# A transformer pair on one Trainium2 core: the last 128 tokens' expert gathers in two halves of 64, and the first half's second block computed together with token block 2

## The chip, the cores and the metric

The program runs on one core of one Trainium2 chip, in float32 throughout. The metric is the device time of one execution in microseconds (us). Before the change it is 1934.56 us, the median of 3 runs (1934.11 to 1935.18).

The engines are named as in the profile: PE (TensorE, the matmuls) and PEld (its weight loads), DVE (VectorE), ACT (ScalarE), POOL (GpSimd, here only the issuer of indirect gathers), SP (SyncE, the issuer of all other transfers).

## The reference, cut to what matters

512 tokens of width 1024 go through two blocks. The first block mixes tokens (attention and a gated recurrence) and then runs a product-key expert layer. The expert layer is what the gathers serve:

```python
def one_block(xb):                                   # 128 tokens
    q = einsum(xb, w_query)                          # 8 heads x 2 x 128
    s = einsum(q, subkeys)                           # scores against 2 x 128 keys
    ... # two top-16 and a top-16 of their 256 sums: 16 experts per head, of 16384
    u = u_table[experts]                             # 128 experts per token, 1024 floats each
    hid = gelu(einsum('nkd,nd->nk', u, xb)) * gates
    return einsum('nk,nkd->nd', hid, v_table[experts])
y = lax.map(one_block, blocks)
```

The second block needs, of each token, the first block's normalised output:

```python
proj = rmsnorm(x) @ w_in        # q, k, v, z_a, u_b, v_b, z_b (512 columns each), g_a, g_b (1024 each)
y_a = stick_breaking_attention(q, k, v) * silu(z_a)     # causal: 8 heads of 64; a token sees earlier ones
y_b = spatial_gating(gelu(u_b), gelu(v_b), ...) * silu(z_b)   # mixes inside 128-token chunks, and the
                                                               # first 64 rows do not see the last 64
x = x + (sigmoid(g_a) * (y_a @ w_up_a) + sigmoid(g_b) * (y_b @ w_up_b)) @ w_out
return rmsnorm(x)
```

## The kernel before, in words

**Token blocks.** The 512 tokens are four blocks of 128, numbered 0 to 3. The first block's mixing runs over the groups `PRE` = (0), (1), (2, 3), the second block over the groups `POST` = (0, 1), (2), (3). A group's weights are loaded once for all its blocks.

**Gathers and batches.** Each token has 128 experts, each with a row of 8 KB in `peer_uv` (1024 floats of u, 1024 of v). One indirect gather (L2313) fetches 128 such rows: one expert slot for 64 tokens on partitions 0 to 63 and another slot for the same 64 tokens on partitions 64 to 127 (the even gathers serve one set of 64 tokens, the odd ones the other). There are 512 gathers, into a ring of 8 buffers (`uv_rows`). Two gathers make a batch: there are 256 batches, numbered 0 to 255, 64 for each token block. A batch is a dot product on DVE for each gather (L2067), a Gelu on ACT (`gelu`), the weights on DVE (`mix`, L2076 and L2077), and 16 records of small matmuls on PE (`rows`, function `weighted_rows`), which accumulate in two PSUM banks `py`. PE's last matmul frees the two ring buffers, and POOL then issues the gathers of four batches later.

**The plan.** `make_plan` writes one list of steps by hand, in ticks of one batch: `dots`, `gelu`, a part of the choice of experts (`tk`, six parts for each head), `mix`, then the tick's steps of dense work, then `rows`. All engines walk this list in order, each doing its part of a step and waiting on semaphores. So a step that PE or DVE waits for holds up everything behind it on that engine. `spread` lays the dense work of the mixing and of the second block over the ticks; `place_keys` adds the projections of the queries for the experts. Expert head g is chosen two heads (16 batches) ahead of its gathers, one head for each 8 batches.

**Where each stage lies.** The second block of group (0, 1) fills batches 133 to 206. Its attention is in batches 159 to 174. The second block of group (2) (`second_rows`) fills batches 207 to 255: projections of 2 weight tiles a batch in 207 to 219, attention units (8, one head each) in 219 to 238, then gates, up projections and the output projection from 239. Steps `out` and `wo` are products that a DVE addition takes out of PSUM (`add_rows`, L1998) in the same tick, behind the tick's `mix`.

**Behind the last gather.** `last_rows(3)` is the second block of token block 3 and has nothing to overlap but itself: `hu` (take block 3's sums out of `py`, scale, transpose), then the projections `q2r`, `k2r`, `v2`, transposes `qt`, `kt`, eight attention units with gates between them, `ua`, `mh`, `wo`, and `fl` (last norm and store).

**Weight tiles.** All dense weights come as tiles of 512 KB (`load_tile`, L832), in the order of the plan. One group of the second block takes 60: `q2` 4, `k2` 4, `v2`, `vb`, `ub`, `zb`, `za` 4 each, `ga`, `gb`, `wo` 8 each, `ua`, `ud` 4 each. There are 4 buffers (`wbuf`); from the first tile of the tail on (`TAIL`) there are 7 more, which lie in the ring. The first tile of the tail waits for the last gather to land, and the 7 wait for ring buffers to come free. A tile of the rows kind (`rows_tile`) is 2 fp32 matmuls of 512 columns for each token block, each shown as 2 records in the profile, so 4 records.

**SP's order.** SP issues tiles, norms and stores in the plan's order and waits for each one's buffer or data.

## Time and profile before

| | before |
|---|---|
| median of 3 runs | 1934.56 us |
| the profiled execution | 1932.01 us |
| its span | 1930.2 us |
| PE / DVE / ACT busy | 1481.9 / 1324.8 / 663.8 us |
| HBM traffic | 377 GB/s over the span |
| granted TensorE clock, mean | 0.871 |

The span runs from the first to the last instruction; the execution's time is 1.8 us longer. Read the profile by stages: the opening without gathers (to about 145 us), the 256 batches (to about 1789 us), and the tail (141 us), in which there is no gather. The share of busy time of an engine is an average over these. In the page's second part the span is cut into 40 slices of 48 us.

### The profile page before, as it was taken

To read this page: it belongs to the slowest core of one execution; us is meant where nothing else is said; L and a number is where in the kernel's file an instruction comes from. 1 tells how busy PE (TensorE), PEld (TensorE's weight loads), DVE (VectorE), ACT (ScalarE), POOL (GpSimd) and SP (SyncE) were. 2 spreads that over 40 slices of the span, in tenths; PEclk is the share of its full clock that TensorE was granted. 3 is DMA by queue.
4 is the path that set the end of the run, shared out by engine and by line. 5 is a ranking of instruction groups with operands and counts; after the bars stand their busy time and mean duration, and the time that the engine had idled before them with its cause. 6 is when DMAs were issued, how large, how long until landed. Compare 5 with 4: busy or idle time off the path is not lost.

```text
span 1930.2 us, 23912 instructions
## 1 busy us (share of the span) xinstructions
PE 1481.9 (77%) x8598; PEld 748.3 (39%) x8598; DVE 1324.8 (69%) x3538; ACT 663.8 (34%) x1236; POOL 609.9 (32%) x529
## 2 busy tenths in 40 slices
PE   7986777668788866866478978688885767767998
PEld 7554443225354433243044434333333222212453
DVE  4357777866788899866876578876766579744332
ACT  3223424243344266132241233521221245311472
POOL 1003323433332343424443333443333334431000
PEclk9989997679888998888599997689997985698999
DMA  7449999999998999999999999999999999999963
GB/s 232 174 155 409 416 417 418 420 417 417 409 408 343 385 418 403 397 417 418 421 407 418 418 418 389 363 406 418 419 418 389 417 418 411 421 417 393 333 233 108
DMA packets 128853, 729.28 MB, mean 378 GB/s; under 512 B 14688, under 2 KB 15872, under 8 KB 63200
## 3 DMA queue, kind: packets, MB, share of 16 engines
q0 software_dynamic: 74272, 537.80, 67.9%
q1 hardware_dynamic: 54464, 189.97, 25.7%
q8 instruction: 68, 1.11, 0.2%
q14 instruction: 49, 0.40, 0.1%
HBM read 725.61 MB, written 2.10 MB: 377 GB/s over the span
## 4 chain that ended last, share of the span: by engine, by line
DMA 34%; PE 31%; DVE 23%; issue 5%; ACT 5%; POOL 2%; SPq 0%; DVEq 0%; POOLq 0%; ACTq 0%
DMA uv_rows<-in_peer_uv,small 24%; PE pa L935 17%; DMA wbuf<-in_wt 11%; DVE uv_rows L2067 8%; PE pb L935 7%; PE py L935 6%; ACT area L1388 2%; ACT L1382 2%; POOL uv_rows L2313 2%; DVE tk L2076 1%; DVE tk L2077 1%; DVE area L2166 1%; DVE small L2054 1%; ACT small L1388 1%; DVE tk L2017 1%
## 5 line engine op out<-in xcount | busy, mean ns | idle before, releaser
L2313 POOL DMA_INDIRECT uv_rows<-in_peer_uv,small x512 | 602.5, 1177 | 1150.9 <-PE py L935 933.9
L2067 DVE CUSTOM_DVE_ANT_0 uv_rows<-uv_rows,xrep 128x1024 f32<-128x1024 f32 x512 | 615.1, 1222 | 228.2 <-DMA uv_rows<-in_peer_uv,small 225.4
L935 PE MATMUL py<-uv_rows,tk 64*32 64x512 f32 x4096 | 349.0, 744 | 301.7 <-DVE tk L2077 301.5
L935 PE MATMUL pa<-wbuf,area 128*128 128x512 f32 (+2 forms) x784 | 346.6, 592 | 44.2 <-DMA wbuf<-in_wt 41.4
L1388 ACT ACTIVATE small<-small 128x2 f32<-128x2 f32 (+4 forms) x327 | 70.3, 216 | 867.8 <-DVE small L2067 842.2
L1382 ACT ACT_TABLE_LOAD x250 | 320.8, 1283 | 5.4 <-DVE small L2199 1.0
L935 PE MATMUL pa<-area,wbuf 128*128 128x256 f32 (+2 forms) x1280 | 238.9, 345 | 27.3 <-DMA wbuf<-in_wt 13.0
L935 PEld LDWEIGHTS pa<-area,wbuf 128*128 128x128 f32 x1280 | 203.9, 200 | 87.0 <-issue 46.1
L935 PEld LDWEIGHTS pa<-wbuf,area 128*128 128x128 f32 (+1 forms) x784 | 135.9, 191 | 255.4 <-issue 178.4
L935 PEld LDWEIGHTS py<-uv_rows,tk 64*32 64x32 f32 x4096 | 50.7, 115 | 447.7 <-DVE tk L2077 401.3
L1388 ACT ACTIVATE area<-pa 128x512 f32<-128x512 f32 (+7 forms) x225 | 88.6, 412 | 229.8 <-PE pa L935 208.5
L935 PE MATMUL pb<-wbuf,area 128*128 128x512 f32 x304 | 146.4, 626 | 20.2 <-DMA wbuf<-in_wt 13.4
L2076 DVE TENSOR_TENSOR tk<-small 128x2 f32<-128x2 f32 x256 | 41.2, 161 | 101.0 <-ACT small L1388 48.9
L935 PEld LDWEIGHTS pb<-wbuf,area 128*128 128x128 f32 x304 | 57.2, 198 | 111.9 <-issue 86.5
L935 PE MATMUL pb<-area 128*128 128x128 f32 (+10 forms) x490 | 98.1, 371 | 1.9 <-DVE area L1871 1.0
L1388 ACT ACTIVATE area<-area 128x512 f32<-128x512 f32 (+3 forms) x104 | 67.5, 655 | 36.1 <-DVE area L1860 25.1
L935 PEld LDWEIGHTS pa<-xnT,wbuf 128*128 128x128 f32 x512 | 64.1, 205 | 28.0 <-issue 18.0
L935 PE MATMUL pa<-xnT,wbuf 128*128 128x128 f32 x512 | 68.6, 293 | 6.6 <-DMA wbuf<-in_wt 4.1
L935 PEld LDWEIGHTS pb<-area 128*128 128x128 f32 (+2 forms) x490 | 64.2, 207 | 24.5 <-issue 19.1
L935 PEld LDWEIGHTS pa<-area 128*128 128x128 f32 (+2 forms) x336 | 54.3, 242 | 39.9 <-issue 33.3
L935 PE MATMUL pa<-area 128*128 128x64 f32 (+3 forms) x336 | 62.7, 345 | 1.8 <-DVE area L1899 0.8
L2077 DVE TENSOR_TENSOR tk<-small,tk 128x64 f32<-128x64 f32 x256 | 57.5, 225 | 8.9
(259 smaller groups left out, 1230.4 us busy)
## 6 DMA issues: line engine op xcount, KB each, us to landing
wbuf<-in_wt SPq DMA_DIRECT2D x300, 512.0 KB, 8.5
uv_rows<-in_wt SPq DMA_DIRECT2D x36, 512.0 KB, 5.8
uv_rows<-in_peer_uv,small POOLq DMA_INDIRECT x512, 14.4
wbuf<-in_skT SPq DMA_DIRECT2D x11, 256.0 KB, 7.4
h<-in_x SPq DMA_DIRECT2D x4, 512.0 KB, 11.5
an<-in_x SPq DMA_DIRECT2D x3, 512.0 KB, 4.7
out<-h SPq DMA_DIRECT2D x3, 512.0 KB, 8.2
area<-in_finw SPq DMA_DIRECT2D x2, 512.0 KB, 9.6
```

Source lines behind the costliest of these rows:

```text
L935: return nc.tensor.matmul(o, l, r, start=start, stop=stop, skip_group_check=True)
L1382: nc.scalar.preload_act_table_set(TABLES[func])
L1388: return nc.scalar.activation(dst, src, func, **more)
L2017: last = V.match_replace(s2[:, a, :], sv[:, a, 0:8], rows[:, a, :], FMIN)
L2054: V.tensor_scalar(gate[to, cols], gexps[tok, g % 2, 1 - m::TG], gsum[tok, g % 2, 1:2], None, ALU.mult)
L2067: last = V.tensor_tensor_reduce(uv_rows[:, n % RING, 0:D], uv_rows[:, n % RING, 0:D], xrep[:, b % 2, n % TG, :], 1.0, 0.0, ALU.mult, ALU.a ...
L2076: step(V.tensor_tensor(wcol[:, k % 2, :], dots[:, at:at + BATCH], gate[:, col:col + BATCH], ALU.mult))
L2077: V.tensor_tensor(mix_w[k % 2], token_mask.unsqueeze(1).broadcast_to([P, BATCH, Q]), wcol[:, k % 2, :].unsqueeze(2).broadcast_to([P, BATCH ...
L2166: step(V.tensor_tensor_scan(rcs[:, 0:wide][:, ::-1], seg2[:, 0:wide], soft[:, 0:wide][:, ::-1], 0.0, ALU.mult, ALU.add))
L2313: nc.gpsimd.indirect_dma_start(uv_rows[:, n % RING, :], None, t["peer_uv"], bass.IndirectOffsetOnAxis(ap=expert_ids[:, c:c + 1].bitcast(U3 ...
```

## The change

* Token block 3 becomes two halves of 64 tokens, numbered 4 and 5 (`HALVES`). `POST` becomes (0, 1), (2, 4), (5).
* The gathers of token block 3 come by halves: batches 192 to 223 fetch all 128 experts of the first 64 tokens, 224 to 255 those of the other 64 (`gather_column`, `tokens_of`, `tokens_at`). The number of gathers, their size and the ring are as before. `weighted_rows` writes 256 columns for each matmul there, and twice as many matmuls; each half has its own 256 columns of the two `py` banks.
* An expert head of token block 3 is now used up in 4 batches (for the first half) and used again for the second. So heads 20 to 31 are chosen one for each 6 batches from batch 142 on (`chosen_part`, `DENSE` = 142) and not one for each 8.
* `late_rows` replaces `second_rows((2,))` for batches 207 to 255 (`LATE` = 49 rows). `q2`, `k2`, `v2` of block 2 (12 tiles) are in batches 207 to 212. At batch 224 (`FIRST_HALF` = 17) the first half's sums are taken (`hu`). From batch 225 there are 2 tiles in each batch: the half's own `q2r`, `k2r`, `v2` (12 tiles) in chunks of 4 that alternate with `vb`, `ub`, `zb`, which serve block 2 and the half together, then `za`, `gb`, `ud`, `ga`, `ua`, `wo` for both. Block 2's eight attention units have their scores in batches 213 to 227, the half's four units theirs in 232 to 238. In all there are 72 tiles here, where there were 60.
* A half's rows product is written with its 512 output columns in two PSUM partition halves: the left 256 columns on partitions 0 to 63, the right 256 on 64 to 127 (`product`). So there are 4 fp32 matmuls of 256 columns for each weight tile, and what follows on DVE and ACT is 128 partitions of 256. An attention unit of a half is two heads of 64 query rows: 4 units and not 8.
* The tail (`last_rows(5)`) has 64 tokens. It has the same 60 weight tiles, and the same 11 buffers.
* `hu` of a half moves 8 quarters of its sums out of PSUM (4 on DVE, 4 on ACT), since the arrangement changes; sums over a row that lies on two partitions are folded by three small DVE instructions (`fold`).
* The additions of `out` and of `wo` for (0, 1) come one batch later, behind the next batch's `dots` and ahead of its `mix` (`adds_behind`).

```diff
-POST = [(0, 1), (2,), (3,)]
+HALVES = (NB, NB + 1)
+POST = [(0, 1), (2, HALVES[0]), (HALVES[1],)]
+LATE = 49
+FIRST_HALF = 17
+def late_rows(g):
+    b, h = g
+    rows = [[] for _ in range(LATE)]
...
+    t = FIRST_HALF + 1
+    scores = {(b, u): 6 + 2 * u for u in range(n_units(b))}
+    turns = {(b, u): 10 + 2 * u for u in range(n_units(b))}
+    values = {(b, u): 12 + 2 * u for u in range(n_units(b))}
+    for u, rows_of_unit in enumerate(((7, 10, 14), (9, 12, 16), (11, 16, 19), (13, 17, 20))):
+        scores[h, u], turns[h, u], values[h, u] = (t + r for r in rows_of_unit)
...
+    put(FIRST_HALF, ("ldhalf",), ("hu", h))
...
+    for i, pair in enumerate(pairs_of(tiles("q2", (b,)) + tiles("k2", (b,)) + tiles("v2", (b,)))):
+        put(i, *pair)
+    steps = []
+    for own, both in (("q2r", "vb"), ("k2r", "ub"), ("v2", "zb")):
+        steps += tiles(own, (h,)) + tiles(both, g)
+    steps += tiles("za", g)
+    for gate, up in (("gb", "ud"), ("ga", "ua")):
+        for c in range(2):
+            steps += tiles(gate, g, c) + [(up, g, c, i) for i in range(2)]
+    for i, pair in enumerate(pairs_of(steps)):
+        put(t + i, *pair)
+    for i, pair in enumerate(pairs_of(tiles("wo", g, 0) + tiles("wo", g, 1))):
+        put(t + 27 + i, *pair)
+    return rows
+DENSE = PER_HEAD * 17 + 6
+def chosen_part(k):
+    if k < DENSE:
+        return k // PER_HEAD + LEAD, k % PER_HEAD
+    return 17 + LEAD + 1 + (k - DENSE) // 6, (k - DENSE) % 6
...
+def adds_behind(rows):
+    rows = [list(row) for row in rows] + [[]]
+    for i, row in enumerate(rows[:-1]):
+        rows[i + 1][0:0] = [("add", s[1], s[2], s[0]) for s in row if s[0] in ("out", "wo") and s[3] == 3]
+    return rows
...
-    spread(second_rows((2,)), 3 * PER_BLOCK + 15, n, ticks)
+    for k, row in enumerate(late_rows(POST[1])):
+        ticks[n - LATE + k] += row
...
-        out += [("dots", k), ("gelu", k)]
+        out += [("dots", k), ("gelu", k)] + [s for s in ticks[k] if s[0] == "add"]
...
+            def product(ps, b, rows_, w, start, stop):
+                if b not in HALVES:
+                    return mm(ps[:, :], rows_, w, start, stop)
+                for q in range(2):
+                    last = mm(ps[side(q), 0:H], rows_, w[:, H * q:H * (q + 1)], start, stop)
+                return last
...
+            def half_rows_up(b):
...
+                for q in range(4):
+                    last = V.tensor_copy(half_rows_at(scratch, b, q, 0), psum_y[0][quarter(q), H * m:H * (m + 1)])
+                last.then_inc(y_copied, 1)
+                dve.wait_ge(y_copied, 2 * m + 2)
+                for c in range(2):
+                    r = cell(b, c)
+                    weights = uv_rows[r, (GATHERS - RING) % RING, W * c:W * (c + 1)] if is_last((b,)) else w1_half[r, :]
+                    V.tensor_tensor(an[r, 0:W], scratch[r, 0:W], weights, ALU.mult).then_inc(u_ready, 1)
...
+        def gather_column(n):
+            if n < GATHERS - SLOTS:
+                return n % (2 * SLOTS)
+            n -= GATHERS - SLOTS
+            return SLOTS * ((NB - 1) % 2) + TOP * (n % (SLOTS // 2) // PER_HEAD) + TG * (n % PER_HEAD) + n // (SLOTS // 2)
```

## Rows read from the trace of the kernel before

**Rows 1.** Page, second part: DMA share (tenths) and rate in 40 slices.
```profile
DMA  7449999999998999999999999999999999999963
GB/s 232 174 155 409 416 417 418 420 417 417 409 408 343 385 418 403 397 417 418 421 407 418 418 418 389 363 406 418 419 418 389 417 418 411 421 417 393 333 233 108
```
**Rows 2.** Stages: us; busy (count) of PE, PEld, DVE, ACT, POOL; clock; DMA; GB/s.
```profile
1184.50:1271.30 86.80, 64.98 (x392) 29.58 (x392) 79.15 (x208) 43.64 (x73) 36.83 (x32) 0.61 0.94 367
1596.80:1674.50 77.70, 59.16 (x336) 23.15 (x336) 72.39 (x191) 39.52 (x73) 36.08 (x30) 0.56 1.01 416
1674.50:1737.00 62.50, 42.59 (x213) 13.23 (x212) 25.11 (x53) 10.76 (x17) 19.69 (x18) 1.00 1.02 417
1737.00:1788.70 51.70, 38.25 (x188) 12.27 (x188) 22.52 (x47) 6.86 (x13) 8.95 (x9) 0.90 0.97 392
1788.70:1930.20 141.50, 128.85 (x416) 64.54 (x416) 43.03 (x59) 67.25 (x113) 0.00 (x0) 0.98 0.61 221
```
**Rows 3.** The chain that ended last: start us, us, what; batches 240 to 255.
```profile
1679.27 13.43 DMA wbuf<-in_wt
1692.74 2.00 PE pa L935 x4
...
1783.84 3.71 PE pb L935 x8
1787.55 1.10 PE py L935 x16
```
**Rows 4.** The same chain in the tail.
```profile
1788.73 0.68 DVE an L2095
...
1792.32 14.00 PE pa L935 x32
...
1922.69 1.73 PE pb L935 x4
...
1926.49 0.72 ACT h L1388
```
**Rows 5.** Page, third and sixth part: bytes by queue, and issues.
```profile
q1 hardware_dynamic: 54464, 189.97, 25.7%
wbuf<-in_wt SPq DMA_DIRECT2D x300, 512.0 KB, 8.5
```
**Rows 6.** As in rows 2, for L2077 alone, one instruction a batch: DVE (count).
```profile
1474.00:1788.70 314.70, 10.80 (x48) 0.83 1.01 411
```
**Rows 7.** What reads or writes `tk`, as in rows 2, without POOL.
```profile
145.00:1788.70 1643.70, 348.95 (x4096) 50.65 (x4096) 395.49 (x1845) 9.57 (x62) 0.86 1.00 408
```
**Rows 8.** Page, fifth part: the mixing weights, part of the above.
```profile
L2076 DVE TENSOR_TENSOR tk<-small 128x2 f32<-128x2 f32 x256 | 41.2, 161 | 101.0 <-ACT small L1388 48.9
L2077 DVE TENSOR_TENSOR tk<-small,tk 128x64 f32<-128x64 f32 x256 | 57.5, 225 | 8.9
```
**Rows 9.** Groups by shape, 50 to 130 us (the opening), PE.
```profile
L935 PE MATMUL pa<-wbuf,area 128*128 128x512 f32 x48 | 21.6, 596 | 0.6 <-ACT area L1388 0.6
L935 PE MATMUL pa<-wbuf,area 128*16 128x512 f32 x32 | 7.6, 595 | 0.0
```
**Rows 10.** What L1998, the additions, waited for: us, times.
```profile
  PE pb L935: 25.4, 8
```
**Rows 11.** SP's issues of tail tiles, in order of time.
```profile
1783.95 3.95 SPq L832 DMA_DIRECT2D wbuf<-in_wt  x4
1787.95 4.16 SPq L832 DMA_DIRECT2D uv_rows<-in_wt  x7
```
**Rows 12.** Two stretches of the tail, as in rows 2.
```profile
1790.00:1810.00 20.00, 19.00 (x52) 8.94 (x53) 4.34 (x9) 7.70 (x22) 0.00 (x0) 1.00 1.02 397
1860.00:1880.00 20.00, 20.00 (x76) 10.76 (x75) 5.21 (x6) 14.64 (x22) 0.00 (x0) 1.00 1.03 412
```
**Rows 13.** Two stretches of the late batches, as in rows 2.
```profile
1500.00:1560.00 60.00, 40.62 (x194) 12.29 (x192) 34.50 (x97) 16.28 (x25) 18.79 (x18) 1.00 1.02 417
1600.00:1660.00 60.00, 44.22 (x262) 16.56 (x261) 56.89 (x154) 36.67 (x65) 28.05 (x24) 0.56 1.01 414
```

More of the change, by code:

```diff
@@ L971, in halves_tile, with transposed_into, quarters @@
                     open_banks.remove(c)
[L973 to L978 removed]
+            def transposed_into(ps, parts, full):
+                for k, part in enumerate(parts):
+                    last = nc.tensor.transpose(ps[:, P * k:P * (k + 1)], part, ident)
+                last.then_inc(full, 1)
+            def quarters(src):
+                n = src.shape[1] // P
+                return [src[:, P * k:P * (k + 1)] for k in range(n)]
             def first_rows(name, i):
@@ new lines, in half_scales @@
+                if is_last((b,)):
+                    scratch = junk
+                else:
+                    scratch = sc_words
+                    act.wait_ge(idx_ready, HP * (NB - 1))
+                for q in range(4):
+                    last = fn(half_rows_at(scratch, b, q, 1), psum_y[1][quarter(q), H * m:H * (m + 1)], ACT.Copy)
+                last.then_inc(y_copied, 1)
+                act.wait_ge(y_copied, 2 * m + 2)
+                step(fn(scratch[:, W:], scratch[:, 0:W], ACT.Square, accum_out=half_ss[:, m, 0:1]))
@@ L1611, in _, with take_quarter_columns @@
+            def take_quarter_columns(dst, ps, end=True):
+                for i in range(2):
+                    last = fn(dst[:, i::2, :], cut(ps[:, P * i:P * (i + 1)], 2, TOK), ACT.Copy)
+                if end:
+                    last.then_inc(a_free, 1)
+            weighed, turned_n = 0, 0
             for s in PLAN:
@@ new lines, in half_input, with half_sums @@
+            def half_input(b):
+                m = half_index(b)
+                dve.wait_ge(scales, m + 1)
+                dve.wait_ge(uv_free, GATHERS - SLOTS // 2 + BATCH)
+                for c in range(2):
+                    for q in range(2):
+                        last = V.tensor_scalar(x1(b)[side(q), c, :], an[cell(b, c), H * q:H * (q + 1)], half_r1[cell(b, c), m:m + 1], None,
+                                               ALU.mult)
+                step(last)
+            def half_sums(b):
+                col = 16 + nth(b)
+                dve.wait_ge(out_sq, 1)
+                fold(ss[:, col:col + 1], ss[:, col:col + 1], out_ss)
```

819 lines of the change are left out of this document (500 added, 319 removed).

## The prediction

> **What bounds the kernel now.** I read the page's slices first. From slice 4 to slice 37 the DMA digits are 9 almost everywhere and the rate is 405 to 420 GB/s, with a few dips (343, 385, 363); then it falls to 333, 233 and 108 [rows 1]. So the batches are bound by bytes at about 418 GB/s, and the tail is not. The view by stages says the same more closely: batches 224 to 247 run at DMA 1.01 to 1.02 and 416 to 417 GB/s while PE and DVE have idle time, and the 141.5 us behind the last gather have DMA 0.61, 221 GB/s, and PE busy 128.85 us of it [rows 2]. The chain of waits confirms both. Late in the batches it consists of waits of 13 us for a weight tile between pieces of PE of 2.00 us [rows 3]: tiles queue behind gathers. In the tail it is PE alone, one tile product after the other, from 1792.32 to 1924.42 us, with a few us of DVE and ACT at either end [rows 4]. One stretch, batches 160 to 175, has another bound: DVE is busy 79.15 of 86.8 us and the DMA rate falls to 367 GB/s [rows 2].
>
> So two rules follow for the batches: a byte more costs time, and work of PE, DVE or ACT costs nothing until one of them is full. For the tail it is the reverse: PE's columns cost time, and bytes are nearly free.
>
> **The change, part by part.**
>
> *12 more weight tiles in the batches.* The late stage has 72 tiles and not 60. A tile is 512 KB = 0.524 MB [rows 5]; 12 are 6.29 MB, at 417 GB/s [rows 2] 15.1 us. The DMA is full there, nothing hides this. Check of the rule on the stage before: 1474 to 1788.7 us holds the last 48 batches [rows 6]; some 45 batches of gathers (four are ahead in the ring) are 94.4 MB, 60 tiles 31.5 MB, together 125.9 MB, at 417 GB/s 302 us of the 314.7. **+15**, bounds +11 (some of it falls in a dip) and +16.
>
> *The choice of experts every 6 batches.* All DVE work on `tk` is 395.5 us [rows 7]; without the mixing weights (41.2 + 57.5 [rows 8]) 296.8 us, 9.3 us for each of 32 heads. In the stretch that DVE bounds, two heads in 16 batches become 16/6 = 2.7: 6.2 us more on an engine with 7.6 us of idle time that it doesn't find in order. I count +6 there, and +2 for the rest of batches 142 to 213, where DVE has room. **+8**, bounds 0 and +30 (all 3.25 heads that come earlier, at 9.3 us). Behind batch 213 DVE gets this time back, where the DMA bounds.
>
> *PE in batches 224 to 255.* DMA: 32 batches of 2.10 MB and 60 tiles are 98.6 MB, 236 us, 7.4 us a batch. PE: a rows tile for 128 tokens has 4 records; in the tail 32 records took 14.00 us, so 1.75 us a tile [rows 4]. For the half, the question is whether the matmuls on two column halves of PE overlap. The trace has this form once, with 16 columns: 32 records of 512 columns on 128*16 were busy 7.6 us, 0.24 each, where 48 records on 128*128 took 21.6 us, 0.45 each [rows 9]. They do overlap, two by two. A half's tile is 8 records of 256 columns, by this 8 x 0.12 = 0.95 us. Changing shape costs something: 16 records of `py`, which on 8 PE tiles are two rounds of 0.43, took 1.10 us [rows 3], so 0.25 for going in and out. A shared tile is then 1.75 + 0.86 + 0.25 = 2.9 us. Sum: 48 x 2.9 + 12 x 1.0 + 32 x 1.15 for `py` + about 20 for attention units and transposes = 208 us of 236, against about half of the time in the batches before [rows 2]. This is close enough that orders and waits begin to show. **+8**, bounds 0 and +30.
>
> The Trainium skill, page TensorEngine Tiling (Array Packing), section Key Properties, says that changing the tiling mode, not just the tile, drains TensorE, and here that would happen twice in each of the 48 shared tiles. The `py` row agrees as far as it goes, with its 0.25 us; by the row this is 12 us of PE time, which is in the 208.
>
> *Taking the first half's sums at batch 224.* PE waits in the plan for DVE's and ACT's copies and scaling; behind it stand that batch's `rows`. As in the tail now, PE stands 3.6 us (1788.73 to 1792.32 [rows 4]), here about 5, and the ring has up to four batches in hand. **+2**, bounds 0 and +6. In batch 255 two shared tiles (5.8 us) stand ahead of the last `py`, where 3.71 us stood [rows 3]. **+2**.
>
> *Additions one batch later.* DVE waited 25.4 us in 8 of them in all [rows 10], parts of it in the tail; most lie where the DMA was full anyway. **-1**, bounds -5 and 0.
>
> *Moves that I cost at nothing.* Gathers by halves: same number, bytes and ring; the expert choice of the last head ends in batch 213, its first gather is issued about batch 216. Twice as many matmuls in `weighted_rows`: the same columns. SP's stores of block 2 move behind the last tiles, they no longer stand ahead of a tile.
>
> Sum up to the last `py`: 15 + 8 + 8 + 4 - 1 = **+34**, own bounds +15 and +60. It ends at 1788.7 + 34 = 1822.7.
>
> *The tail.* Now 141.5 us: 60 tiles of 1.75 us are 105, the rest is ends and attention. After: `hu` takes 5 us (4 quarter copies of about 0.4, two scalings of 0.69 [rows 4], transposes, two more). PE then needs 60 x 0.95 = 57 us for tiles and about 12 for four units (half of the present 128.85 - 105), 69 us. The weights need more: seven of the first eleven tiles are issued 0.7 us ahead of the end of `py` now (1787.95 against 1788.65 [rows 3, 11]); while tiles flow freely the rate is 397 to 412 GB/s [rows 12], 1.3 us a tile, so the last of the remaining 56 tiles lands at about 56 x 1.28 + 1 = 73 us. Then its product (1), and the end: from PE's last record to the end of the span it is 5.8 us now (1924.42 to 1930.2 [rows 4]); halves are cheaper on DVE and ACT but `fold` adds three small instructions, 7. I add 3 us where the last unit's values, `ya`, `yo` and `ua` follow one another with few tiles between them: **84 us**, -57.5. Bounds 78 (tiles at 417 GB/s, no gap) and 100 (PE, its ends and the chain of the units added up, not overlapped).
>
> Together: +34 - 57.5 = -23.5. The profiled execution of 1932.0 (span 1930.2 + 1.8) becomes 1908.5; the median of the runs is 2.5 above the profiled one: **1911 us**.
>
> **The rivals.**
>
> *A. PE becomes the bound of batches 224 to 255 at the low clock (slower).* From 1596.8 to 1674.5 us the granted clock was 0.56 of full speed, mostly the lower of its two levels (1.2 GHz), with attention units and `py` on PE and no tiles; from 1500 to 1560, with tiles and fewer attention units, it was 1.00 at 2.4 GHz, although PE was busy less [rows 2, 13]. The new stage mixes both: units beside two tiles a batch. At the low level a shared-tile batch is 2 x 5.5 + 2.2 = 13 us against 7.4 by bytes. For: PE already has 88% of the stage at full speed. Against: PE full of tile products kept 1.00 throughout the tail [rows 12]. From 6 such batches on (5.7 us each) the gain is gone; with 9, +51 instead of +8: 1954 us. Chance 0.13.
>
> The Trainium skill, page TensorE: Matmul & The Clock Gate, section "What's actually happening", makes it a matter of how busy PE was; by that a fuller PE would stay at speed. The two stretches of rows 13 differ from this: 74% busy was granted 0.56, 68% busy 1.00.
>
> *B. Halves on PE don't overlap with 64 columns each.* Then the tail's tiles cost what they cost now; only the attention halves, tail 141.5 - 12 = 129; and PE in batches 224 to 255 gets 60 x 0.8 = 48 us more, 256 of 236 us, +20. 1911 + 45 + 20 = 1976. Against it stands the 128*16 row [rows 9]. Chance 0.03.
>
> *C. DVE bounds batches 142 to 213.* For: 91% busy in 160 to 175 [rows 2]. All 30 us appear: +22 over my sum, 1933. Chance 0.08.
>
> *D. The tail is a chain, not a flow of bytes.* In-order waits between units, gates and 3 PSUM banks keep it at 98 to 100 us: 1926. Chance 0.11.
>
> **How the numbers follow.** The forecast has 0.65 and a range of its own from 1889 (+17, 80) to 1929 (+45, 91); A to D have 0.35. Below 1888 everything would have to be at its good bound; 0.1. Above 1940 lie A's worse part and B, 0.1. So 1888 to 1940. What can be told from no change is 0.2%, 3.9 us. Slower by more than that: A nearly whole, B, a little of C: 0.17. Within it: parts of C, A and D: 0.06. Faster: 0.77.
>
> **What would show it.** Right: about 72 tile issues over the last 49 batches at 415 to 418 GB/s, the last `py` at 1815 to 1835 us; records of 128*64 with 256 columns, about 0.12 us of busy time each; a tail of 80 to 92 us with DMA share over 0.85 and PE waiting for tiles. The clock decides A: under 0.8 over ten batches with PE over 95% busy and DMA under 0.95. Wrong in a step: DMA rate under 400 between batches 142 and 213 with DVE over 90% (C); idle PE and idle DMA together in the tail (D). If the last `py` comes after 1850 us or the tail is over 105 us, the forecast is wrong.

## The result, and the profile after

The changed kernel takes 1922.29 us (median of 5 runs, 1920.67 to 1925.43) where the kernel before takes 1934.11: a ratio of 0.9943, 95% interval 0.993 to 0.9956. The forecast was 1911. The direction was right, the size was half: 11.8 us and not 23.5. The profiled execution has a span of 1918.9 us against 1930.2, 11.3 less.

The page of the kernel after, second part (DMA share and rate in 40 slices), third and sixth part (bytes of the queue and issues); it answers to [rows 1, 5]:

```profile
DMA  7549999999998999999999999999999999999997
GB/s 223 185 152 410 416 417 418 421 416 417 403 414 348 389 418 407 385 419 416 421 407 405 417 418 400 349 392 418 418 413 402 392 420 375 416 370 383 395 375 284
q1 hardware_dynamic: 56672, 196.52, 26.7%
wbuf<-in_wt SPq DMA_DIRECT2D x312, 512.0 KB
```

There are 12 tiles more (6.29 MB), as the diff says; the queue moved 6.55 MB more in all. The tail's last slices went from 333, 233, 108 to 395, 375, 284 GB/s. But of the four slices before them, three are now at 375, 370 and 383, where they were at 411, 417 and 393 in [rows 1]: something other than bytes slows the late batches.

The view by stages of the kernel after: us; busy (count) of PE, PEld, DVE, ACT, POOL; clock; DMA; GB/s. The rows are batches 160 to 175, batches 208 to 223, a slice of 10 us, and the stretches between two places explained below (1666.6, and the end of the last `py`, 1827.7, which the rows round to 1827.8) and the end:

```profile
1185.30:1274.70 89.40, 68.58 (x392) 31.79 (x392) 84.93 (x231) 44.24 (x75) 35.92 (x32) 0.56 0.95 357
1487.40:1581.00 93.60, 63.54 (x694) 34.23 (x678) 63.07 (x150) 36.83 (x70) 39.34 (x34) 0.74 1.01 406
1590.00:1600.00 10.00, 10.00 (x143) 5.44 (x128) 5.74 (x17) 8.19 (x15) 4.09 (x4) 0.91 0.64 222
1666.60:1827.80 161.20, 155.50 (x1300) 69.13 (x1300) 77.54 (x160) 44.33 (x84) 36.94 (x34) 0.99 0.96 377
1827.80:1918.90 91.10, 72.85 (x624) 45.68 (x624) 32.98 (x67) 41.84 (x89) 0.00 (x0) 0.93 0.87 340
```

The last `py` comes 39 us later than before (1827.7 against 1788.6), and the tail is 91.1 us in place of 141.5, 50.4 less. 39.1 - 50.4 = -11.3.

Where the 39 come from is read off the instruction that makes the mixing weights, one a batch (L2371, before L2077). Its counts up to the first tenth of a us that has the 209th and the 225th of them, first before, then after:

```profile
145.00:1482.90 1337.90, 46.74 (x209) 0.86 1.00 407
145.00:1596.60 1451.60, 50.41 (x225) 0.86 1.00 408
```

```profile
145.00:1487.50 1342.50, 46.92 (x209) 0.85 1.00 406
145.00:1581.10 1436.10, 50.54 (x225) 0.85 1.00 406
```

The 209th (batch 208) starts at 1482.9 before and 1487.4 after, +4.6; the 225th (batch 224) at 1596.5 and 1581.0, -15.5, because 16 tiles fewer are loaded between (16 x 0.524 MB at 417 GB/s = 20.1 us, just the difference). From batch 224 to the last `py` it is 192.1 us before and 246.7 after, +54.6. The bytes of 28 more tiles, priced as in the forecast, are 35.2; **19.4 us are left**, where the forecast had 12 (8 + 2 + 2). This split is one by the forecast's own terms: it does not show that the bytes cost 35.2.

The chain that ended last, of the kernel after, around 1666 us: start us, us, what.

```profile
1662.89 0.69 DVE sc L2481
1663.60 0.74 DVE sc L2482
1664.37 0.69 DVE small L2483
1665.08 0.31 ACT small L1628
...
1666.61 7.54 PE pa L1155 x24
1674.15 1.02 PE py L1155 x32
...
1819.77 1.02 PE py L1155 x32
1820.80 5.86 PE pb L1155 x24
1826.65 1.11 PE py L1155 x32
```

At 1666.6 us (the first product of `zb`, batch 235) PE has waited 3.5 us for ACT, and ACT for the layer norm's statistics on DVE. From there on the chain is PE alone, 161 us with 5.6 us of small gaps: two shared tiles in 5.86 us, `py` in 1.02, the next two tiles. PE is busy 155.5 of 161.2 us there, while the DMA moves 377 GB/s. 161.2 us at 377 GB/s are 60.8 MB, at the 416 of free flow 146 us: by this estimate PE costs 15 us in this stretch. A pair of shared tiles, 2.94 us each, is what the forecast had (2.9). Its sum was right and its place wrong: it compared 208 us of PE with 236 us of DMA over the whole stage, but the heavy batches stand together at the end.

The tail in the same chain:

```profile
1827.84 0.41 DVE uv_rows L2403
...
1831.05 1.13 PE pb L1204 x4
...
1833.02 9.32 PE pa L1155 x64
...
1857.20 4.49 PE pa L1155 x40
1861.71 10.84 DMA wbuf<-in_wt
1872.59 2.01 PE pa L1155 x24
...
1887.72 0.63 ACT area L1628
1888.35 0.34 ACT uv_rows L1628 x2
...
1888.73 3.60 PE pb L1155 x16
...
1898.52 3.67 PE pb L1155 x32
...
1907.68 1.97 PE pb L1155 x16
...
1914.16 0.51 ACT h L1628
```

`hu` takes 5.2 us as forecast, and the forecast flow of tiles is there too: from 1838 to 1898 the DMA is full, and the last tile is issued at 1899.65. But PE's last record ends at 1911.4 (its last record on this chain, at 1909.65), not 1 us behind the last tile; from there to the end of the span it is 7.5 us, where the forecast had 7. What PE waited for in the tail, the largest and the waits for tiles (us in total, times, longest):

```profile
PE pb L1204 <- DVE an L2409: 3.4, 1, 3.4
PE pb L1155 <- ACT uv_rows L1628: 3.3, 2, 2.7
PE pb L1155 <- ACT area L1628: 2.2, 3, 1.1
...
PE pa L1155 <- DMA wbuf<-in_wt: 0.2, 1, 0.2
```

PE hardly waits for a tile: 0.2 us. The chain above has a DMA piece of 10.84 us all the same. That piece names what released PE last; PE itself was busy 10.00 of 10 us in the slice 1858 to 1868. So the page leaves open which of the two, PE's order or the bytes, sets the tail, and the same question stands for the stage before. The experiments are about these two.

The wait of 3.4 us behind the last `py` has a second price. The clock that was granted to PE behind it, in the kernel after, and at the same place in e12 (an experiment below in which this wait is gone):

```profile
1830.70:1837.50 6.80, 5.60 (x26) 3.30 (x28) 2.94 (x10) 2.39 (x9) 0.00 (x0) 0.50 1.02 413
```

```profile
1824.50:1845.00 20.50, 16.20 (x130) 8.60 (x132) 3.33 (x12) 6.40 (x19) 0.00 (x0) 1.00 1.00 390
```

0.50 is the lower of the two levels, 1.2 GHz. The first 64 records of the tail's tiles took 9.32 us there, where 64 like them at full clock took 7.06 (both in the chain above and under e6).

### The profile page after: what moved, and what is told of

It reads as the page before. It is cut to its first block, busy times and chain, and to the rows that moved or that the text cites. A ratio compares the mean times of both kernels' runs of the same rounds, so it can differ in the third digit from the quotient of the medians.

```text
span 1918.9 us, 27896 instructions
## 1 busy us (share of the span) xinstructions
PE 1497.6 (78%) x10478; PEld 792.3 (41%) x10478; DVE 1344.7 (70%) x3627; ACT 677.2 (35%) x1293; POOL 601.3 (31%) x530
## 4 chain that ended last, share of the span: by engine, by line
PE 36%; DMA 29%; DVE 22%; issue 6%; ACT 6%; POOL 2%; DVEq 0%; SPq 0%; POOLq 0%; ACTq 0%
DMA uv_rows<-in_peer_uv,small 24%; PE pa L1155 19%; PE pb L1155 9%; DVE uv_rows L2360 7%; PE py L1155 7%; DMA wbuf<-in_wt 5%; ACT area L1628 2%; ACT L1622 2%; POOL uv_rows L2662 2%; DVE tk L2370 1%; DVE tk L2371 1%; DVE area L2512 1%; ACT small L1628 1%; DVE small L2347 1%; DVE tk L2308 1%
## 5 line engine op out<-in xcount | busy, mean ns | idle before, releaser
L1155 PE MATMUL py<-uv_rows,tk 64*32 64x512 f32 (+1 forms) x5120 | 342.2, 618 | 286.3 <-DVE tk L2371 284.5
L1155 PE MATMUL pa<-wbuf,area 128*128 128x512 f32 (+3 forms) x1200 | 379.6, 516 | 29.2 <-DMA wbuf<-in_wt 18.5
L1628 ACT ACTIVATE small<-small 128x2 f32<-128x2 f32 (+5 forms) x338 | 73.1, 218 | 850.7 <-DVE small L2360 800.3
L1155 PEld LDWEIGHTS pa<-wbuf,area 128*128 128x128 f32 (+2 forms) x1200 | 155.0, 171 | 248.7 <-issue 206.8
L1628 ACT ACTIVATE area<-pa 128x512 f32<-128x512 f32 (+8 forms) x240 | 88.2, 394 | 219.8 <-PE pa L1155 207.8
L1155 PE MATMUL pb<-wbuf,area 128*128 128x512 f32 (+1 forms) x400 | 151.4, 563 | 15.6 <-DMA wbuf<-in_wt 5.6
L1155 PE MATMUL pb<-area 128*128 128x128 f32 (+14 forms) x522 | 100.2, 370 | 2.2 <-ACT area L1628 1.1
L1628 ACT ACTIVATE area<-area 128x512 f32<-128x512 f32 (+4 forms) x104 | 66.9, 650 | 36.1 <-DVE area L2152 25.5
L1155 PEld LDWEIGHTS pb<-area 128*128 128x128 f32 (+4 forms) x522 | 62.3, 196 | 26.1 <-issue 20.5
L1155 PE MATMUL pa<-area 128*128 128x128 f32 (+5 forms) x400 | 65.4, 319 | 1.8 <-DVE area L2191 0.8
L2371 DVE TENSOR_TENSOR tk<-small,tk 128x64 f32<-128x64 f32 x256 | 57.7, 225 | 9.0 <-DVE tk L2370 0.2
```

The costliest lines, as they stand in the source:

```text
L1155: return nc.tensor.matmul(o, l, r, start=start, stop=stop, skip_group_check=True)
L1628: return nc.scalar.activation(dst, src, func, **more)
L2371: V.tensor_tensor(mix_w[k % 2], token_mask.unsqueeze(1).broadcast_to([P, BATCH, Q]), wcol[:, k % 2, :].unsqueeze(2).broadcast_to([P, BATCH ...
```

## The experiments

Medians of the kernel before moved between 1931.9 and 1935.6 us from one comparison to the next, so ratios to it carry the comparison. The kernel after has 0.9943 (0.993 to 0.9956). A difference of medians is given below only for orientation.

A single profiled execution has noise of its own, and it lies mostly ahead of the stages in question: in the kernel after and thirteen experiments the plan is the same up to batch 208, and yet this batch comes between 1481.9 us (e10) and 1490.1 us (e9). So stages are compared by their length inside one execution. Starts are those of the mixing weights' instruction, as above; the `zb` place is where PE waits for ACT, at 1666.6 in the kernel after. All in us:

| | start of batch 208 | batch 224 to the `zb` place | `zb` place to the last `py` | the two together | tail |
|---|---|---|---|---|---|
| kernel after | 1487.4 | 85.6 | 161.1 | 246.7 | 91.1 |
| e5 (the same plan to the last `py`) | 1489.7 | 84.5 | 161.1 | 245.6 | 90.4 |
| e6 (the same plan to the last `py`) | 1486.4 | 85.8 | 161.6 | 247.3 | 140.2 |
| e1 | 1485.5 | 83.0 | 163.2 | 246.2 | 89.6 |
| e2 | 1487.3 | 83.6 | 150.6 | 234.2 | 91.0 |
| e7 | 1486.1 | 84.2 | 163.7 | 248.0 | 89.6 |
| e8 | 1484.7 | 86.2 | 160.0 | 246.2 | 89.5 |
| e13 | 1485.0 | 83.0 | 159.6 | 242.5 | 90.9 |
| e15 | 1490.0 | 80.3 | 159.3 | 239.7 | 90.3 |
| e11 | 1486.9 | 87.8 | 163.9 | 251.8 | 90.9 |

The first three rows show how far the same plan repeats: within 1.7 us for the two together. Behind the `zb` place e1, e7 and e11 have 7.9 to 9.4 us at the lower clock level and the others of the table 3.4 to 5.2; their busy time there is 2.2 to 2.9 us above that of the kernel after, which is the whole difference of these lengths.

### Batches 224 to 255: bytes or PE?

**e1**: the 12 own tiles transfer a sixteenth of their bytes.

```diff
+                if s[0] in ("q2r", "k2r", "v2") and s[1] == (HALVES[0],):
+                    slot, src = slot[:, 0:64], src[:, 0:64]
                 sp.dma_start(slot, src).then_inc(w_full[SPOTS[n]], 16)
```

> The changed kernel, but the 12 weight tiles that only the first half uses (q2r, k2r, v2 of group (4)) are loaded as 32 KB and not 512 KB each; the rest of their buffers holds old data. All other work is as in the changed kernel (1922 us). Theory BYTES (the late batches are bound by the DMA rate, as the sum assumed): 5.9 MB less at 417 GB/s, 14 us less, about 1908. Theory PE (from the first shared tiles on, batches 226 to 255 are paced by PE: two shared tiles 5.9 us, py 1.0 us and the attention units): the tiles lie in chunks between shared ones and the DMA catches up elsewhere in the stage, so under 7 us less, 1916 to 1921.

Measured: 1916.29 us, ratio 0.9907 (0.989 to 0.9923); span 1915.0. Twelve tiles are 15 us by bytes; 6.0 came back by the medians. The profile doesn't show them where the tiles are loaded: 2.6 us less up to the `zb` place, 2.1 more behind it, 0.5 in sum. Both say that most of the 15 us was not paid.

**e2**: PE's work for the first half in the 48 shared tiles cut to half.

```diff
-                    for k in range(2):
+                    n_k = 1 if g == POST[1] and g[j] in HALVES else 2
+                    for k in range(n_k):
```

> The changed kernel, but in the 48 tiles that block 2 and the first half share, the first half's product leaves out the second 128 rows of each tile: 96 column-half pairs of 0.43 us less on PE, some 20 us of PE time between batches 226 and 255, all loads as before. Theory BYTES: 0 to 3 us less, 1919 to 1922. Theory PE: batches 232 to 247, 8.8 us each in the changed kernel against 7.4 by bytes, come down to about 8.0; the last py ends 8 to 14 us earlier, 1908 to 1914.

Measured: 1907.79 us, ratio 0.987 (0.9849 to 0.9891), span 1906.1. No byte is gone, and 14.5 us are. The waited-for place before the PE stretch is at 1664.48 and not 1666.61; the last `py` ends at 1815.1 and not 1827.8. So 10.5 of the 12.7 us came from the stretch behind that place, where 40 shared tiles lost 0.4 us each: PE's busy time there fell by 16.7 us, and PE waited 5.7 us for tiles, where it had not waited for one (from 1690 to 1760 us the DMA is back at 416 GB/s). This is far outside the 1.7 us of the table: PE's work sets this stretch, with the bytes 10 to 15 us behind it.

**e7**: the first half's sums in two steps. PE's transposes, and DVE's taking of the columns, move from batch 224 to the start of batch 225 (a new step `ht`); PE still waits for the copies out of `py` before it writes there. Two places of the edit:

```diff
+    rows[t][0:0] = [("ht", h)]
...
-                elif name == "hu":
+                elif name == "ht":
                     pe.wait_ge(u_ready, 2 * half_index(s[1]) + 2)
```

> After, but the first half's sums are taken in two steps: the transposes on PE and the taking of columns by DVE move from batch 224 to the start of batch 225, so that in batch 224 PE goes on with that batch's products while ACT and DVE copy; only the fold stays. The kernel after shows DMA at 222 GB/s in 1590 to 1600 us, POOL waiting 11 us for PE: about 4.7 us lost there. HU-STALL theory: 2 to 4 us less than after (1918 to 1920), the slices around 1590 us at 400 GB/s or more. Rival (PE has no slack behind that place either, what it gains there it gives back in 1690 to 1760 us, where it is full): within 1 us of after.

Measured: 1916.88 us, ratio 0.9901 (0.9883 to 0.9919). In the kernel after PE waited 9.4 us at this place, more than the 5 of the forecast; now 6.0 + 0.9. The first line is the kernel after, the second e7 (engine, tile, waited for: us in total, times, longest):

```profile
PE pb L1204 <- DVE an L2409: 9.4, 1, 9.4
```

```profile
PE py L1156 <- DVE sc L2406: 6.0, 1, 6.0
```

The slice at 1590 us went from 222 to 301 GB/s, not to the 400 that was expected. The gain of the runs (5.4 us by the medians, more than expected) lies outside the interval of the kernel after, but e7's own profiled execution (span 1918.5) is the slowest of its four runs and doesn't show where it went: 1.4 us less up to the `zb` place, 2.6 more behind it. Only the wait is shown.

**e8**: in every second shared tile the two blocks change places, so that fewer changes of shape stand between them.

```diff
-                for j, ps in enumerate(open_banks):
+                blocks = list(enumerate(open_banks))
+                if g == POST[1] and i % 2 == 0:
+                    blocks = blocks[::-1]
+                for j, ps in blocks:
```

> After, but every second shared tile takes its two blocks in reverse order (first half's small products first or last), so that two tiles that follow one another change between full-width and column-half records two times fewer per pair: half of the changes of shape go. Shared tiles cost 2.94 us each on PE in the kernel after, 0.36 above 1.75 + 0.83 by records without a change. SWITCH theory (those 0.36 us are the changes of shape): 48 x 0.12 to 0.18 = 6 to 9 us less PE time in the stage, of which the 20 batches bound by PE give back 3 to 5 us: 1917 to 1919. Rival (the 0.36 us are weight loads and waits between records, not the change): shared tiles stay at 2.9 us and the time within 1 us of after.

Measured: 1916.47 us, ratio 0.9898 (0.9878 to 0.9918), span 1914.4. The same pair of tiles on PE, kernel after and e8 (start us, us, engine, line, operation, tiles, shape of the first record, count):

```profile
1710.31 5.93 PE L1155 MATMUL pa<-wbuf,area 128*128 128x512 f32 x24
```

```profile
1708.26 5.73 PE L1155 MATMUL pa<-wbuf,area 128*64 128x256 f32 x24
```

0.20 us a pair, for one change of shape fewer inside it (two in place of three). 24 pairs are 4.8 us, and the runs gained 5.8 by the medians. That the one is the cause of the other is not shown: in the stage itself the profile has 0.5 us less. Behind the `zb` place PE's busy time fell by 2.3 us, and PE waited 1.1 us for a tile, where it had not. The Trainium skill, page TensorEngine Tiling (Array Packing), section Key Properties, says that changing the tiling mode drains TensorE. These lines agree with it as far as they go, with 0.2 us a change here.

**e13**: e7 and e8 together (both diffs).

> After, with the first half's sums in two steps and the turned block order, the last shared tiles where they were. Alone the two edits gave 5.4 and 5.8 us. If PE's work and PE's waits between batch 224 and the last py are one sum that sets the end, both count: 10 to 11 us less than after, 1911 to 1912.5. If the stage has a second bound close behind (bytes: 19.3 us of surplus over the bytes of 28 tiles, less what the units of block 2 hide), they share: 6 to 8 us less, 1914 to 1916.

Measured: 1915.13 us, ratio 0.991 (0.9897 to 0.9924), span 1912.2. The two gains of 5.4 and 5.8 don't add up: 7.2 by the medians, and 4.2 in the stage (246.7 to 242.5).

**e15**: e13 with e1's small own tiles.

> The kernel of e13 (first half's sums in two steps, turned block order), and the half's own 12 tiles transfer 32 KB each, as in e1. Against after e1 gave 6.0 us, e7 5.4, e8 5.8, e13 (the edits of e7 and e8 together) 7.2. TWO-BOUNDS theory for batches 224 to 255 (PE's sum and the bytes stand side by side; e13 left PE little above the bytes): with 12 x 1.25 = 15 us of bytes gone behind it, both gains show in full, 10 to 14 us less than e13: 1901 to 1905. Rival (both draw on one and the same slack, the ring's four batches): at most 4 us less than e13, 1911 to 1915.

Measured: 1914.49 us, ratio 0.9913 (0.9896 to 0.993), span 1912.7. The theory of two bounds side by side fails for this stage: 10 to 14 us were expected, and the runs give 0.6 against e13, inside the intervals. The stage is 2.8 us shorter than in e13 (242.5 to 239.7), nearly what the same small tiles gave up to the `zb` place in e1; that e15's span isn't shorter is because this execution was 5.0 us behind e13's at batch 208 already, where nothing differs. The traces say where the rest went. The first `zb` product in e13 and in e15:

```profile
1661.66 8.22 PE L1156 MATMUL pa<-wbuf,area 128*64 128x256 f32 x24 [4.05 <-ACT area L1634]
```

```profile
1663.05 7.94 PE L1158 MATMUL pa<-wbuf,area 128*64 128x256 f32 x24 [3.97 <-ACT area L1636]
```

Four of the own tiles' products lie just ahead of this place, and at this place PE waits 4 us for ACT in both. ACT waits for a chain on DVE that begins with the mixing weights of batch 233 and goes through an attention unit and two layer norms. The two ends of it in e15 (the start, to compare with the 1663.05 above):

```profile
1647.06 0.22 DVE L2379 TENSOR_TENSOR tk<-small,tk 128x64 f32<-128x64 f32 x1
```

This is 16.0 us; it is 16.0 to 16.4 in the kernel after and in every experiment that keeps the order of the tiles, and 17.4 in e11. A tile that lands sooner inside these 16 us gives nothing, since PE must wait for the chain anyway; only what is saved before batch 233 counts. So the stage has three pieces in series: one up to batch 233, to which `hu`, PE's tiles and bytes contribute; 16 us of DVE and ACT; and one of 161 us, which shrinks by more than 2 us only where the shared tiles themselves cost PE much less (e2).

**e11**: own tiles first, shared tiles behind.

```diff
-        steps += tiles(own, (h,)) + tiles(both, g)
+        steps += tiles(own, (h,))
+    for both in ("vb", "ub", "zb"):
+        steps += tiles(both, g)
```

> After, but the half's own 12 tiles (q2r, k2r, v2) come all ahead of the first 12 shared ones (vb, ub, zb) and not in turns by four: the same tiles, bytes and PE work in batches 225 to 236, in another order. Theory (PE and DMA both nearly full; in turns, batches with 2 us and with 5.9 us of tile products on PE average out over the four batches of the ring): own first gives six batches bound by bytes with PE at rest, then six with PE at 9 us a batch against 7.4 by bytes, 6 x 1.5 = 9 us more less what the ring and the attention units of block 2 absorb: 2 to 6 us slower than after, 1924 to 1928. Rival (these batches are bound by DVE and ACT in the units of block 2, or by bytes throughout, whatever the order): within 1 us of after.

Measured: 1925.8 us, ratio 0.9964 (0.9952 to 0.9977), span 1923.9. By the medians taking turns is worth 3.5 us, but the interval overlaps that of the kernel after (its upper end is 0.9956), so the runs alone don't settle it. In the profile the `zb` place comes 2.2 us later behind batch 224; the 2.8 us more behind it go with the longer time at the lower clock level.

### Batches up to 224: the choice and the additions

**e3**: the kernel before, with the heads from 20 on chosen in 6 batches each.

```diff
+def chosen_part(k):
+    if k < DENSE:
+        return k // PER_HEAD + LEAD, k % PER_HEAD
+    return 17 + LEAD + 1 + (k - DENSE) // 6, (k - DENSE) % 6
...
-        g = k // PER_HEAD + LEAD
+        g, part = chosen_part(k)
```

> The kernel before, with only the choice of experts moved: heads 20 to 31 one for each 6 batches from batch 142. The sum priced this at +8 us (bounds 0 and +30). The trace of the changed kernel shows some 3 us gained on the kernel before's pace between batches 160 and 200. Theory DVE (the stretch 160 to 175 passes every us on): +5 to +8 us, 1939 to 1942. Theory cover (most of it falls in waits, and what is moved away from batches 214 to 237 gives a little back): 0 to +3 us, 1934 to 1937.

Measured: 1937.81 us, ratio 1.0025 (1.0013 to 1.0037): 2.5 to 7.2 us slower, 4.5 by the medians. The term was +8. In e3's profile batch 208 comes 8.0 us later than in the kernel before (1490.9 against 1482.9) and the last `py` 5.9 us later; the noise of one execution at batch 208 is of this size.

**e4**: the kernel after, with the additions in their own batch again (the line is shortened, and further places of the edit are left out).

```diff
-        rows[i + 1][0:0] = [("add", ...) for s in row if s[0] in ("out", "wo") and s[3] == 3]
+        rows[i] = [t for s in row for t in ([s, ("add", ...)] if s[0] in ("out", "wo") and s[3] == 3 else [s])]
```

> The changed kernel with the additions of out and of wo for (0, 1) back in the tick of their product. The sum priced the move at -1 us (bounds -5 and 0). Theory bytes-bound: no difference, within 1 us of 1922. Rival (DVE held up by the additions sets when ring buffers come free): 2 to 5 us slower, up to 1927, with later mixing weights around batches 40, 108 and 203.

Measured: 1925.01 us, ratio 0.9966 (0.9947 to 0.9985), span 1923.2, with batch 208 at 1492.9 us and not 1487.4. The intervals overlap, so the runs alone don't settle it. The profile makes the move worth more than the 1 us of the forecast: 1492.9 lies 2.8 us above the latest of the fourteen kernels that have the additions one batch later, and 5.5 above the kernel after.

### The tail: bytes or PE's order?

**e5**: all tiles that are loaded in the tail transfer a sixteenth.

```diff
+                if n >= TAIL:
+                    slot, src = slot[:, 0:64], src[:, 0:64]
                 sp.dma_start(slot, src).then_inc(w_full[SPOTS[n]], 16)
```

> After, but all weight tiles that are loaded in the tail transfer 32 KB each in place of 512 KB (first 64 columns); PE's work and every wait stay. The tail is 91.1 us in the profiled execution (last py 1827.8, end 1918.9). FLOW theory (the DMA carries the tail at 406 to 410 GB/s for 71 us, and what comes behind it is short): with the bytes gone the tail falls to PE's own sum, about 5 for hu, 60 x 1.16 = 69 with the units beside, 9 for the end: 78 to 82, so 9 to 13 us less than the kernel after, about 1910. CHAIN theory (in-order waits between units, banks and tiles set the order anyway, the loads only fill the gaps): the tail stays at 87 to 91, 1918 to 1922. Up to the last py nothing changes (1827 to 1828).

Measured: 1922.16 us, ratio 0.9931 (0.9912 to 0.9949), span 1919.4: no change. The middle of the tail and the whole of it in e5, columns as in the stages above:

```profile
1838.00:1898.00 60.00, 55.34 (x504) 35.93 (x500) 21.84 (x35) 33.88 (x61) 0.00 (x0) 0.97 0.12 27
1829.00:1919.40 90.40, 72.32 (x624) 46.03 (x624) 32.97 (x67) 41.86 (x89) 0.00 (x0) 0.93 0.14 33
```

27 GB/s in place of 408, and PE does in 60 us what it did before (55.0 us busy there in the kernel after). The flow of bytes, by which the forecast priced the tail, doesn't set it; whether it stands close behind is the question of e12 and e14.

**e6**: in the tail, both column halves to the same 64 partitions. The right half's output is thus not formed.

```diff
-                    last = mm(ps[side(q), 0:H], rows_, w[:, H * q:H * (q + 1)], start, stop)
+                    last = mm(ps[side(0), 0:H] if b == HALVES[1] else ps[side(q), 0:H], rows_, ...)
```

> After, but in the tail the products of both column halves of a tile go to the same 64 partitions of the bank, so that no two of them can run beside one another (the sums of the second half of the output columns aren't formed). If column halves overlap two by two as the prediction took from the 128*16 row, a tile of the tail goes from about 1.16 us on PE to 8 records of 0.22 to 0.25, 1.8 to 2.0 us, and the tail from 91 to about 60 x 1.9 + 12 for units + 5 + 9 = 130 to 145 us: 1958 to 1976 in all. If they had never overlapped (rival B), nothing changes: 1922. Up to the last py nothing changes.

Measured: 1971.05 us (one run), span 1969.3. The chain in the kernel after, then in e6, for the same 64 records (8 tiles):

```profile
1849.02 7.06 PE pa L1155 x64
```

```profile
1860.52 13.96 PE pa L1155 x64
```

0.88 us a tile against 1.75: two products of 64 rows by 256 columns do run beside one another, fully. Without it, in the tail alone, the changed kernel would be 35 us slower than the one before (1971.05 against 1935.62 in the same comparison; the one run is far outside what runs differ by).

**e9**: the last two shared tiles behind the last `py`, so that PE works while DVE copies.

```diff
+    wo = [s for s in ticks[n - 1] if s[0] == "wo"]
+    out = [s for s in out if s not in wo] + wo
```

> After, but the last two shared tiles (of the output product wo) stand on PE behind the last py and not ahead of it. In the kernel after they take 5.86 us ahead of the last py (1820.80 to 1826.65), and behind it PE stands 3.4 + 0.8 us while DVE copies the sums. PE-ORDER theory (PE is the bound of the last batches, so the last py comes 5.9 us earlier, and PE's idle time behind it is filled): 4 to 5 us less, 1917 to 1918.5; the tail then begins near 1822 and is 1 to 2 us longer. BYTES theory (the last py waits for gathers that landed at 1816.9 and for its weights anyway, the tail ends with its last tile, whose load is not issued earlier): within 1 us of after, 1921.5 to 1923.

Measured: 1923.28 us, ratio 0.9945 (0.9932 to 0.9958). No gain, and the profile shows a new wait; DVE in e9 (last column: idle before, and what ended it):

```profile
1830.55 0.69 DVE L2630 TENSOR_TENSOR h<-h,pb 128x512 f32<-128x512 f32 x1 [7.02 <-PE pb L1157]
1831.64 0.42 DVE L2630 TENSOR_TENSOR h<-h,pb 128x256 f32<-128x256 f32 x1 [0.41 <-PE pb L1157]
1832.09 1.72 DVE L2405 COPY uv_rows<-py 32x256 f32<-32x256 f32 x4
```

The additions of the moved tiles stand ahead of the copies in DVE's order. They waited for PE, the copies waited behind them, and then PE waited 3.8 us for the copies, now behind the tiles.

**e10**: e7, e8 and e9 together.

> After, with the three edits at once: sums of the first half in two steps, block order turned in every second shared tile, last two shared tiles behind the last py. If each gave back PE time at the same bound (PE between batch 224 and the end), they add until the bytes bound again: 5.4 + 5.8 + 4.5 = 15.7 less than after, 1906.5; the bytes of the stage allow it (28 more tiles by bytes would be 35 us where after has 54, so 19 us of surplus). If two of them only fill the same slack of the ring of gathers: 8 to 11 us less, 1911 to 1914.

Measured: 1917.92 us (1913.64 to 1921.6), ratio 0.9919 (0.9905 to 0.9934). This is outside both ranges that were expected. The last `py` ends 12.5 us earlier than in the kernel after, but 5.9 of these are the two moved tiles and 4.5 were there at batch 224 already. The tail, with the two moved tiles in it, is 96.6 us: e9's wait is in it.

**e12**: e10 with DVE's order mended.

```diff
+    h = HALVES[1]
+    rest = [s for s in flat(last_rows(h)) if s not in (("hu", h), ("ht", h))]
+    return first + out + [("hu", h)] + wo + [("ldlast",), ("ht", h)] + rest
```

> The kernel with all three edits, but with DVE's order mended: DVE's copies of the last half's sums stand ahead of its additions of the last wo tiles, the columns from PE behind them. In e9 and e10 DVE stood 7.0 and 6.6 us at the additions, waiting for the tiles that had moved behind the last py, and the copies stood behind them, so PE's 3.8 us of waiting came back after the tiles. DVE-ORDER theory: PE's wait behind the last py goes (3.8 to under 1 us), the tail falls from 96.7 to 91 to 93 us, span 1906 to 1908, and the runs lie 4 to 5 us under those of e10: 1913. Rival (what lengthened the tail in e9 and e10 is the tail's later loads or the PE work itself, 5.9 us moved across the border and nothing saved): within 1 us of e10, 1917 to 1919.

Measured: 1913.48 us, ratio 0.9905 (0.9891 to 0.992), span 1916.0 (the profiled execution is above the median of its runs). The diff leaves out e7's, e8's and the lines that take `wo` out. PE in e12, from the last `py` on:

```profile
1818.18 5.73 PE L1160 MATMUL pb<-wbuf,area 128*64 128x256 f32 x24
1823.84 0.66 PE L1212 MATMUL pb<-ident,an 128*128 128x128 f32 x4
1825.41 3.67 PE L1160 MATMUL pa<-wbuf,area 128*64 128x256 f32 x32 [0.92 <-DVE area L2429]
...
1836.44 1.08 PE L1160 MATMUL pa<-uv_rows,area 128*64 128x256 f32 x8 [1.37 <-DMA uv_rows<-in_wt]
```

The 3.4 us behind the last `py` are gone, as expected, and with them the 6.8 us at the lower clock level. The tail is 97.8 us all the same, 92.1 beside the moved tiles' 5.7, where 91 to 93 in all were expected: PE now waits for tiles, 3.8 us in 14 waits, where it waited 0.2.

**e14**: e12 with e5's small tiles in the tail.

> The kernel of e12 (PE no longer waits for DVE behind the last py), and all weight tiles that are loaded in the tail transfer 32 KB in place of 512 KB. In e5 taking away the bytes alone gave nothing; in e12 taking away PE's wait alone left the tail at 92 us beside the moved tiles, and PE waited for tiles at 1831 to 1839 us instead. TWO-BOUNDS theory (PE's chain and the flow of bytes through the tail are within 1 to 2 us of one another, each hides the other's gain): with both gone the gain of PE's order shows, 3 to 5 us less than e12: span 1911 to 1913, runs 1908.5 to 1910.5. Rival (the tail's length comes from something that neither touches): as e12, 1913 to 1914.

Measured: 1909.65 us, ratio 0.9885 (0.9868 to 0.9901), span 1909.1. The tail is 90.2 us, 84.5 beside the moved tiles. Taking away the bytes alone gave nothing (e5), PE's wait alone gave nothing (e12: 92.1 against 91.1), both gave 6.6 to 7.6 us. Against e5 (90.4), 3.3 us of it are waits of PE and 2.6 us are busy time, with 3.4 us at the lower clock level in place of 10.2. In the tail two bounds do stand side by side. The profiles show this, where tails of the same plan lie between 89.4 and 91.1; the intervals of the runs of e12 and e14 still touch.

Of the kernels that leave nothing out, e7, e8, e10, e12 and e13 all stand at 0.99, below both kernels; their intervals don't tell them from one another.

## Why the prediction was half right

Point by point, in its own terms:

- **+15, 12 more tiles.** The bytes are there (6.29 MB). But the term assumed that bytes bind to the end. Without them e1's runs are 6 us faster and its stage is 0.5 us shorter; e15 against e13 has 0.6 and 2.8. So at most 6 of the 15 us were paid by bytes, and the rest is hidden behind PE's work and the chain on DVE.
- **+8, the choice; -1, the additions.** The choice alone measured +4.5 (2.5 to 7.2), with +8.0 at batch 208 in its profile; the additions, by the profile, more than -1. Together they are +4.6 at batch 208 against +7. Rival C's condition was near: DVE was busy 84.9 of 89.4 us in batches 160 to 175. Still the choice cost some 5 us and not 30.
- **+8, PE in batches 224 to 255, with +2 for `hu` and +2 for batch 255.** This is the first step that was mis-sized: 19.4 us of surplus in place of 12. The price of a shared tile was right (2.94 against 2.9), that of `hu` half of it (PE waits 9.4 us, not 5). The failure is that 208 of 236 us was taken as an average over the stage. The light batches come first; behind them stand 16 us of DVE and ACT, and then 161 us in which PE is busy 155.5, and in which e2 gave back 10.5 us for less work of PE and no byte less. The comparison with the kernel before was also misread: PE was busy 68 to 76% there [rows 2], not about half.
- **Sum up to the last `py`: +34, measured +39**, within its own bounds of 15 to 60. That it came so near owes something to luck: the first part was 2.4 us too dear, the stage behind it 7.4 too cheap.
- **Tail: 84, measured 91.1.** The second mis-sized step. The forecast had 5 for `hu`, 69 for PE and 7 for the ends, 81 in sum, and a flow of tiles of 73 us; it took the larger flow, with 3 us for waits between the last unit, `ya`, `yo` and `ua`. The flow is there and doesn't set the time alone (e5). Measured are 5.2, 78.3 and 7.5. The 78.3 are 6.6 us of waits, 4.2 of them in the place named, and 71.7 of PE's work; 2.3 us of this are the lower clock behind PE's wait in `hu`, a cost that the forecast had at nothing. These waits lie in PE's own way, since no tiles are left in its order to fill them. So the step that failed is to let PE's sum stand beside the flow of bytes without its waits and its clock.
- **The overlap of column halves** (against rival B) is shown by e6.
- **Rival A** fails: the granted clock was 0.99 in PE's 161 full microseconds, its upper level of 2.4 GHz. It was 0.56 in batches 160 to 175, as 0.61 before. **Rival D** named the tail's mechanism, waits in order between units, at twice its price.

12 - 19.4 and 84 - 91.1 are 14.5 us too little; the first part of the batches gave 2.4 back. So 11.4 us of the forecast's 23.5 are left, which is the 11.3 of the spans.

## What to carry to other kernels

Where one engine is at 88% of another over a stage, lay out both by batch and look for the place where all engines meet: behind the last such wait, the heavier batches decide alone. Where two resources have nearly the same sum, removing either shows nothing; an experiment that takes both away shows whether they were the only two (e14: 6.6 us came back) or whether a third stands behind them (e15: 2.8 us came back for 15 us of bytes, with the chain on DVE and ACT still there). Compare stages by their length inside one execution: a difference of a few us at a moment counted from the start may have arisen where nothing was changed. Before work is moved into another engine's idle time, read what stands behind it in the order of the engine that consumes it (e9).

## What the runs showed of the hardware

Matmuls of 128 rows to 64 columns of PE, 256 columns wide in fp32: eight records of them, in pairs on different column halves, took 0.88 us, and one after the other 1.75, so the pairing lost nothing. A change between full-width and half-width records cost 0.2 us. Behind an idle PE of 3.4 us the granted clock was 0.50 for 6.8 us (in e1, e4 and e8 for 3.4) and then 1.00 again; in e12, without this idle time, it stayed at 1.00. And a piece of DMA in the chain that ended last (10.84 us) stood beside a PE that was full: the chain names the last releaser, and only a run without the bytes told that it wasn't the bound.
